# The loop over pairs of experts as a hardware loop on four engines instead of four written-out copies

## Chip, core and metric

The kernel runs on one core of a Trainium2 chip. The metric is the device time of one execution in microseconds (us), as the median of repeated runs. TensorE does the matrix products, VectorE and ScalarE the elementwise work, SyncE issues nearly all transfers; GpSimd does nothing here. Each engine has its own instruction stream, and the streams meet only in semaphores.

## The reference, cut to what matters here

The program is a two-layer backbone. What the change touches is the last part of the second layer, a mixture of experts: each of 256 tokens goes to the two best of eight experts, each with three weight matrices of 1024 x 2816 in fp32.

```
def moe_swiglu(h, router, w_gate, w_up, w_down):
    hf = h.reshape(-1, d)                                   # 256 x 1024
    top_v, top_i = lax.top_k((hf @ router), 2)
    top_w = jax.nn.softmax(top_v, axis=-1)
    gates = sum(one_hot(top_i, 8) * top_w[..., None], axis=1)
    y = zeros_like(hf)
    for e in range(8):
        y = y + gates[:, e:e + 1] * (silu(hf @ w_gate[e]) * (hf @ w_up[e])) @ w_down[e]
    return y
```

Everything ahead of it (modulation, gMLP and pooling mixer, dense SwiGLU, two attentions) and the final RMSNorm are the same in both kernels.

## The kernel before

Each fp32 operand is split in two parts, hi and lo, so that one product is three matmuls of fp32r operands: hi x hi, hi x lo, lo x hi (`product`, lines 502 to 506). Weights travel as slabs of 128 x 2048 fp32, 1 MB each. A slab passes four engines:

- SyncE issues its transfer into one of six `raw` buffers (`load`, line 427; the transfer is line 438). It waits for the `lo_ready` semaphore, which says that the slab six places earlier has been split.
- ScalarE copies `raw` to one of three `hi` buffers (`split_hi`, line 451). It waits for the transfer (`raw_in`) and for `slab_used`, which TensorE raises when it is through with the slab three places earlier.
- VectorE subtracts to make `lo` (`split_lo`, line 459), waiting for `hi_ready`, and raises `lo_ready`.
- TensorE waits for `lo_ready` (`slab`, line 466) and does its 12 matmuls (24 for the two narrow slabs of an expert).

An expert is 33 slabs: 22 for the gate and up projections in six column chunks (`features`), 11 for the down projection (`down_e`). In between, TensorE gathers the tokens of the next expert, turns the activations, and scatters the results of the expert before (`gather_rows`, `turn`, `scatter`); ScalarE and VectorE empty those banks. Tokens are gathered into 128 slots for each expert. A ninth pass, `expert("ninth", ...)`, takes the expert whose tokens overflow the 128 slots, whichever that is: its number is read from memory into a register, so SyncE's addresses in it are computed. After that a loop `Fori(0, OVER - 1)` with an `If` inside would take further overflows; with these inputs its body is skipped both times. Its body holds one expert.

Two tables, `slab_order` and `bank_order`, say for each stage how often it is repeated and which count every semaphore reaches. For the stage "moe" they hold one body of two experts (66 slabs), repeated NE // 2 = 4 times. All waits are written with the turn `it`: the count is a constant plus `it` times what one body adds, as in line 469, `there = n0 // SPL + 1 + it * (per // SPL)`. In the kernel before, `it` is a Python number, so every count is a constant in the program, and the body stands there four times for each engine. Where `it` is a register, `load` adds one wait more (lines 434 to 436), for `hi_ready` against a constant:

```
                sp.wait_ge(lo_ready[freed[1] % SPL], freed[1] // SPL + 1 + it * (per // SPL))
                if not isinstance(it, int):

                    sp.wait_ge(hi_ready, freed[1] + 1)
```

VectorE also uses the number of the expert as an address: line 1356 reads a column of `posn`, line 1415 one of `gate_e`.

Of the kernel before, what the change touches and what calls it, by code (L numbers as in the profile page):

```python
# [50 lines left out]
NE = 8  # L51
# [177 lines left out]
def build(nc, a, out):  # L229
# [38 lines left out]
    with ExitStack() as ctx:  # L268
# [158 lines left out]
        def load(sp, stage, key, src, it=0):  # L427

            _, per, slot, _, _, freed = slabs[stage, key]
            if freed and freed[0] == "direct":  # L430
                sp.wait_ge(direct_done, freed[1] + 1)
            elif freed:
# [4 lines that stand above are left out]
            _, k, f = src.shape  # L437
            sp.dma_start(view(raw[slot], (k, f)), src).then_inc(raw_in[slot], 16)
# [20 lines left out]
        def split_lo(dve, stage, key, size=SLAB, it=0):  # L459

            n0, per, slot, _, _, _ = slabs[stage, key]
            dve.wait_ge(hi_ready, n0 + 1 + it * per)
            nc.vector.tensor_tensor(lo[n0 % SPL][:, 0:size], raw[slot][:, 0:size], hi[n0 % SPL][:, 0:size].bitcast(F32),  # L463
                                    ALU.subtract).then_inc(lo_ready[n0 % SPL], 1)
# [32 lines left out]
        def await_emptied(eng, stage, key, it=0, lag=0):  # L497

            b, r, per = banks[stage, key][:3]
            eng.wait_ge(bank_emptied[b], r + 1 - lag * per + it * per)  # L500
# [71 lines left out]
        def _(sp):  # L572
# [53 lines left out]
            def expert(stage, w, e, it):  # L626
                for s, (kind, _, ks, fs) in enumerate(ES):
                    load(sp, stage, (w, s), mw[kind][bass.ds(e, 1), :, ks, fs].rearrange("e p k f -> p (e k) f"), it)
            for it in range(NE // 2):
                for w in range(2):  # L630
                    expert("moe", w, it * 2 + w, it)
            sp.wait_ge(routed, 1)
# [12 lines left out]
        def _(act):  # L645
# [215 lines left out]
            def gathered(stage, w, it=0):  # L861

                for h in range(2):
                    gathered_hi(stage, w, h, it)
                for h in range(2):
                    gathered_lo(stage, w, h, it)
                gathered_places(stage, w, it)
# [15 lines left out]
            def expert(st, w, it):  # L883

                for s in range(33):
                    split_hi(act, st, (w, s), it=it)
                    if s == 2 and st == "moe":
                        out_hi(st, 1 - w, it, lag=1 - w)
                    if s == 2 and st == "ninth":
                        out_hi("moe", 1, NE // 2 - 1)  # L890
                    if s % 4 == 0 and 4 <= s <= 20:
                        silu_e(st, w, s // 4 - 1, it)
                    if s in (10, 14, 18, 22, 24):
                        act_hi(st, w, (s - 10) // 4 if s < 24 else 4, it)
                    if s == 23:
                        silu_e(st, w, 5, it)
                    if s in (25, 26) and st == "moe":
                        gathered_hi(st, w, s - 25, it)
                    if s == 27:
                        act_hi(st, w, 5, it)  # L900
                    if s in (28, 29) and st == "moe":
                        gathered_lo(st, w, s - 28, it)
                    if s == 30 and st == "moe":
                        gathered_places(st, w, it)
            gathered("first", 1)
            for it in range(NE // 2):
                expert("moe", 0, it)
                expert("moe", 1, it)
            expert("ninth", 0, 0)
# [17 lines left out]
        def _(dve):  # L927
# [468 lines left out]
            def act_lo(st, w, c, first, it):  # L1396
                n_ = 4 if c < 5 else 2
                b = full(dve, st, ("t", w, c), it)
                hi_there(st, first + c, it)
                emptied(V.tensor_tensor(aTl[:, 4 * c:4 * c + n_, :], b[:, 0:n_ * P].rearrange("p (k s) -> p k s", k=n_),  # L1400
                                        aTh[:, 4 * c:4 * c + n_, :].bitcast(F32), ALU.subtract), st, ("t", w, c))
# [16 lines left out]
            def expert(st, w, it):  # L1418

                first = {"moe": 8 * w + 2, "ninth": 8 * NE + 2, "over": 0}[st]  # L1420
                for s in range(33):
                    splits(st, (w, s), it=it)
                    if s == 2 and st == "moe":
                        out_lo(st, 1 - w, it, 8 * w, lag=1 - w)
                    if s == 2 and st == "ninth":
                        out_lo("moe", 1, NE // 2 - 1, 16)
                    if s in (6, 10, 14, 18, 22):
                        act_e(st, w, (s - 6) // 4, it)
                    if s in (6, 7) and st != "over":
                        add_out(st, w, it * 2 + w if st == "moe" else NE, range(2 * s - 12, 2 * s - 10), it)  # L1430
                    if s in (10, 14, 18, 22, 24):
                        act_lo(st, w, (s - 10) // 4 if s < 24 else 4, first, it)
                    if s == 12 and st == "moe":
                        place(0, 1 - w, it * 2 + (w + 1))
                    if s == 23:
                        act_e(st, w, 5, it)
                    if s == 27:
                        act_lo(st, w, 5, first, it)
            for it in range(NE // 2):
                expert("moe", 0, it)  # L1440
                expert("moe", 1, it)
            expert("ninth", 0, 0)
# [36 lines left out]
        def _(pe):  # L1479
# [391 lines left out]
            def expert(st, w, it):  # L1871
                if st == "over" or w == 1:
                    for key in (("xl", 1 - w, 1), ("pt", 1 - w)):
                        await_emptied(pe, st, key, it)
                elif st == "moe":
                    for key in (("xl", 1, 1), ("pt", 1)):
                        await_emptied(pe, st, key, it, lag=1)
                else:
                    for key in (("xl", 1, 1), ("pt", 1)):
                        await_emptied(pe, "moe", key, NE // 2 - 1)  # L1880
                for c in range(6):
                    features(st, "g", w, c, it)
                    features(st, "u", w, c, it)
                    if c == 0 and st == "moe":
                        for h in range(2):
                            await_emptied(pe, st, ("d", 1 - w, h), it, lag=1 - w)
                        scatter(st, w, 1 - w, it)
                    if c == 0 and st == "ninth":
                        for h in range(2):
                            await_emptied(pe, "moe", ("d", 1, h), NE // 2 - 1)  # L1890
                        scatter(st, 0, 1)
                    if c:
                        turn(st, w, c - 1, it)
                down_e(st, w, it)
# [4 lines left out]
            gather(0, "first", 1, 0, 2)  # L1899
            for key in (("xl", 1, 1), ("pt", 1)):  # L1900
                await_emptied(pe, "first", key)
            for it in range(NE // 2):
                expert("moe", 0, it)
                expert("moe", 1, it)
            expert("ninth", 0, 0)
# [34 lines left out]
```

## Time and profile before

| | |
|---|---|
| median of 3 runs | 1822.49 us (1821.17 to 1822.96) |
| the profiled execution | 1821.17 us, of which its span, first to last instruction, is 1819.4 us |
| mean granted TensorE clock | 0.958 of full speed |
| busy | TensorE 93%, VectorE 76%, ScalarE 50% |
| DMA | 426 MB, mean 234 GB/s |
| the stage of the change | about 901.6 to 1797 us: eight experts, then the ninth pass |

The times in a row are microseconds from the start of the span, unless marked ns. PE is TensorE's matmuls, PEld its weight loads, DVE VectorE, ACT ScalarE, SP SyncE. PEldq, ACTq, DVEq and SPq are what the sequencers of TensorE, ScalarE, VectorE and SyncE do themselves: branches, register arithmetic, semaphore waits that stand alone, issues of transfers. They are not counted as busy. A matmul's recorded duration overlaps the next one's; what a matmul takes in a stream is the distance of two starts.

### The profile page before, as it was taken

How to read it: one execution, taken by the hardware profiler on the slowest of the kernel's cores; microseconds unless marked ns; L12 is line 12 of the kernel's file. 1: busy time of each engine (PE TensorE's matmuls, PEld its weight loads, DVE VectorE, ACT ScalarE, POOL GpSimd, SP SyncE). 2: the span in 40 equal slices, each digit the busy share in tenths (PEclk: the TensorE clock that was granted, in tenths of full speed). 3: DMA queues.
4: the chain of work that ended last, by engine and by line, in shares of the span. 5: the costliest groups of instructions: out<-in, count | busy, mean ns of one | idle time of the engine just before them, and what ended most of it. 6: DMA issues, size and time to landing. Idle time of an engine off the chain costs nothing.

```text
span 1819.4 us, 20970 instructions
## 1 busy us (share of the span) xinstructions
PE 1689.4 (93%) x8417; PEld 1387.7 (76%) x8418; DVE 1388.9 (76%) x1442; ACT 910.9 (50%) x837; POOL 0.2 (0%) x4
## 2 busy tenths in 40 slices
PE   4988999999999797797799999999999999999995
PEld 1876777788888596466688888888888888888884
DVE  5858657776777845674488988889798989888896
ACT  5431232211122334332477777777677777777773
POOL 0000000000000000000000000000000000000000
PEclk9988999999999898899699999999999999999998
DMA  9533334444567132100299999999999999999992
GB/s 352 195 136 126 113 127 149 139 163 161 170 223 242 53 117 70 47 1 24 68 337 342 358 346 343 358 337 360 344 341 350 354 335 357 341 348 356 334 366 88
DMA packets 214552, 426.32 MB, mean 234 GB/s; under 512 B 8186, under 2 KB 64028, under 8 KB 214452
## 3 DMA queue, kind: packets, MB, share of 16 engines
q1 hardware_dynamic: 210218, 420.37, 65.9%
q10 hardware_dynamic: 4234, 4.57, 0.8%
q8 instruction: 69, 1.13, 0.3%
q14 instruction: 31, 0.25, 0.0%
HBM read 423.86 MB, written 1.05 MB: 234 GB/s over the span
## 4 chain that ended last, share of the span: by engine, by line
PE 88%; DVE 6%; ACT 2%; issue 1%; DMA 1%; SPq 1%; DVEq 0%; ACTq 0%
PE bank L504 26%; PE bank L506 25%; PE bank L505 25%; PE bank L1740 2%; PE bank L1795 2%; PE bank L1729 2%; DVE lo L463 2%; PE bank L1834 1%; PE bank L1515 1%; DMA raw<-in_ada_w_dram 1%; PE bank L1746 1%; PE bank L1509 1%; ACT hi L457 1%; PE bank L1868 0%; PE bank L1869 0%
## 5 line engine op out<-in xcount | busy, mean ns | idle before, releaser
L463 DVE TENSOR_TENSOR lo<-raw,hi 128x2048 fp32r<-128x2048 f32 x361 | 820.8, 2282 | 199.4 <-ACT hi L457 198.0
L457 ACT ACTIVATE hi<-raw 128x2048 fp32r<-128x2048 f32 x361 | 689.7, 1912 | 474.9 <-PE bank L506 454.3
L504 PE MATMUL bank<-hi,xgh 128*128 128x512 f32 (+1 forms) x864 | 328.8, 381 | 5.0 <-DVE lo L463 5.0
L506 PE MATMUL bank<-hi,xgl 128*128 128x512 f32 (+1 forms) x864 | 325.3, 377 | 0.0
L505 PE MATMUL bank<-lo,xgh 128*128 128x512 f32 (+1 forms) x864 | 325.3, 377 | 0.0
L504 PEld LDWEIGHTS bank<-hi,xgh 128*128 128x128 f32 x864 | 163.0, 189 | 36.6 <-issue 5.2
L506 PEld LDWEIGHTS bank<-hi,xgl 128*128 128x128 f32 x864 | 163.1, 189 | 33.0
L505 PEld LDWEIGHTS bank<-lo,xgh 128*128 128x128 f32 x864 | 163.1, 189 | 31.3
L504 PE MATMUL bank<-hi,aTh 128*128 128x512 f32 x396 | 159.0, 402 | 0.0
L506 PE MATMUL bank<-hi,aTl 128*128 128x512 f32 x396 | 154.7, 391 | 0.0
L505 PE MATMUL bank<-lo,aTh 128*128 128x512 f32 x396 | 154.4, 390 | 0.0
L1023 DVE SCALAR_TENSOR_TENSOR acc<-raw,cs,acc 128x512 f32<-128x512 f32 x216 | 146.6, 746 | 1.4
L504 PE MATMUL bank<-Hhi,hi 128*128 128x512 f32 x352 | 140.6, 399 | 2.8 <-issue 2.8
L506 PE MATMUL bank<-Hhi,lo 128*128 128x512 f32 x352 | 138.8, 394 | 0.0
L505 PE MATMUL bank<-Hlo,hi 128*128 128x512 f32 x352 | 138.5, 393 | 0.0
L506 PEld LDWEIGHTS bank<-hi,aTl 128*128 128x128 f32 x396 | 74.3, 188 | 16.6
L504 PE MATMUL bank<-hi,Hhi 128*128 128x256 f32 (+1 forms) x256 | 83.2, 325 | 2.7 <-DVE lo L463 2.7
L505 PEld LDWEIGHTS bank<-lo,aTh 128*128 128x128 f32 x396 | 74.6, 188 | 13.9
L504 PEld LDWEIGHTS bank<-hi,aTh 128*128 128x128 f32 x396 | 74.5, 188 | 13.6
L505 PE MATMUL bank<-lo,Hhi 128*128 128x256 f32 (+1 forms) x256 | 81.3, 318 | 0.0
L506 PE MATMUL bank<-hi,Hlo 128*128 128x256 f32 (+1 forms) x256 | 81.3, 318 | 0.0
L504 PEld LDWEIGHTS bank<-Hhi,hi 128*128 128x128 f32 x352 | 66.6, 189 | 17.8 <-issue 3.7
(315 smaller groups left out, 2188.8 us busy)
## 6 DMA issues: line engine op xcount, KB each, us to landing
raw<-in_moe_w_gate_dram SPq DMA_DIRECT2D x99, 1024.0 KB, 5.9
raw<-in_moe_w_up_dram SPq DMA_DIRECT2D x99, 1024.0 KB, 6.0
raw<-in_moe_w_down_dram SPq DMA_DIRECT2D x99, 1024.0 KB, 6.3
raw<-in_ada_w_dram SPq DMA_DIRECT2D x48, 1024.0 KB, 5.8
raw<-in_ffn_w_gate_dram SPq DMA_DIRECT2D x11, 1024.0 KB, 5.3
raw<-in_ffn_w_up_dram SPq DMA_DIRECT2D x11, 1024.0 KB, 5.3
raw<-in_ffn_w_down_dram SPq DMA_DIRECT2D x11, 1024.0 KB, 5.0
raw<-in_ab_w_in_dram SPq DMA_DIRECT2D x6, 1024.0 KB, 8.7
```

The costliest lines, as they stand in the source:

```text
L457: nc.scalar.activation(hi[n0 % SPL][:, 0:size], raw[slot][:, 0:size], ACT.Copy).then_inc(hi_ready, 1)
L463: nc.vector.tensor_tensor(lo[n0 % SPL][:, 0:size], raw[slot][:, 0:size], hi[n0 % SPL][:, 0:size].bitcast(F32), ALU.subtract).then_inc(lo_r ...
L504: nc.tensor.matmul(dst, lh, rh, start=first, stop=False, skip_group_check=True)
L505: nc.tensor.matmul(dst, lh, rl, start=False, stop=False, skip_group_check=True)
L506: return nc.tensor.matmul(dst, ll, rh, start=False, stop=last, skip_group_check=True)
L1023: ins = V.scalar_tensor_tensor(out=sum_, in0=w_, scalar=c_, in1=biased[:, place_, :] if h == 0 and i < 2 else sum_, op0=ALU.mult, op1=ALU.add)
L1509: filled(T.matmul(bank(pe, st, ("bc", cb, who))[:], ones[:], sums[:, who, :], start=True, stop=True), st, ("bc", cb, who))
L1515: ins = T.matmul(b[:, 2 * j + who:2 * j + who + 1], sums[:, who, j * P:(j + 1) * P], ones[:, 0:1], start=True, stop=True)
L1729: filled(T.matmul(bank(pe, "att", ("s", i))[:], q_, k_, start=True, stop=True), "att", ("s", i))
L1740: ins = T.matmul(b[:, 0:64], pT[:, i % 2, t * P:(t + 1) * P], val, start=(t == 0), stop=(t == 3))
L1746: ins = T.transpose(b[:, t * P:(t + 1) * P], pexp[:, (i - 1) % 2, t * P:(t + 1) * P], ident[:])
L1795: ins = T.matmul(b[:, kk * P:(kk + 1) * P], src[:, t, k * P:(k + 1) * P], Pm[:, par, t, :], start=(t == 0), stop=(t == 1))
```

## The change

In four places, one for each engine, `for it in range(NE // 2)` becomes a hardware loop over the same body. `it` is then a register. The order of the work, the buffers and the semaphores are the same.

```
             def expert(stage, w, e, it):
                 for s, (kind, _, ks, fs) in enumerate(ES):
                     load(sp, stage, (w, s), mw[kind][bass.ds(e, 1), :, ks, fs].rearrange("e p k f -> p (e k) f"), it)
-            for it in range(NE // 2):
+            with sp.Fori(0, NE // 2) as it:
                 for w in range(2):
                     expert("moe", w, it * 2 + w, it)
...
             gathered("first", 1)
-            for it in range(NE // 2):
+            with act.Fori(0, NE // 2) as it:
                 expert("moe", 0, it)
                 expert("moe", 1, it)
...
-            for it in range(NE // 2):
+            with dve.Fori(0, NE // 2) as it:
                 expert("moe", 0, it)
                 expert("moe", 1, it)
...
                 await_emptied(pe, "first", key)
-            for it in range(NE // 2):
+            with pe.Fori(0, NE // 2) as it:
                 expert("moe", 0, it)
                 expert("moe", 1, it)
```

## Rows read from the trace of the kernel before

**Rows 1.** The page's part on busy time, share of the span and instructions, TensorE

```profile
PE 1689.4 (93%) x8417; PEld 1387.7 (76%) x8418; DVE 1388.9 (76%) x1442; ACT 910.9 (50%) x837; POOL 0.2 (0%) x4
```

**Rows 2.** Stretches: length, busy us (xinstructions) PE to POOL, clock, DMA share, GB/s

```profile
999.40:1099.10 99.70, 99.70 (x486) 82.78 (x485) 85.69 (x54) 71.72 (x53) 0.00 (x0) 1.00 0.98 348
...
1103.30:1302.70 199.40, 199.40 (x969) 165.60 (x968) 171.37 (x107) 143.53 (x104) 0.00 (x0) 1.00 0.98 348
```

**Rows 3.** Who waited for whom from 899 to 1797 us: total us, times, longest

```profile
ACT hi L457 <- PE bank L506: 249.4, 283, 3.4
...
PE bank L504 <- DVE lo L463: 5.0, 1, 5.0
```

**Rows 4.** Timeline of TensorE's weight loads at the end of the sixth expert

```profile
1499.24 0.19 PEld L504 LDWEIGHTS bank<-hi,aTh 128*128 128x128 f32 x1
...
1501.96 0.19 PEld L504 LDWEIGHTS bank<-hi,xgh 128*128 128x128 f32 x1
```

**Rows 5.** Lines 470 and 477: ns min/median/max, first and last start in us

```profile
L470 PEldq EVENT_SEMAPHORE  x1: 51/51/51, 1498.6 to 1498.6; - x1
...
L477 PEldq EVENT_SEMAPHORE  x1: 51/51/51, 1498.7 to 1498.7; - x1
```

**Rows 6.** Timeline of ScalarE and VectorE in the same stretch

```profile
1494.28 1.92 ACT L457 ACTIVATE hi<-raw 128x2048 fp32r<-128x2048 f32 x1 [0.80 <-PE bank L506]
1497.00 1.92 ACT L457 ACTIVATE hi<-raw 128x2048 fp32r<-128x2048 f32 x1 [0.80 <-PE bank L506]
...
1496.23 2.29 DVE L463 TENSOR_TENSOR lo<-raw,hi 128x2048 fp32r<-128x2048 f32 x1 [0.43 <-ACT hi L457]
1498.95 2.29 DVE L463 TENSOR_TENSOR lo<-raw,hi 128x2048 fp32r<-128x2048 f32 x1 [0.43 <-ACT hi L457]
```

**Rows 7.** Branch and register instructions at lines 1912 and 1910, TensorE's queue

```profile
L1912 PEldq COMPARE_BRANCH  x2: 221/2082/3944, 1800.1 to 1805.4; - x2
...
L1910 PEldq FUSED_REGOPS  x2: 59/59/59, 1799.1 to 1804.6; - x2
L1910 PEldq ALU_OP  x2: 36/39/42, 1804.1 to 1805.7; - x2
L1910 PEldq COMPARE_BRANCH  x2: 76/159/242, 1804.3 to 1805.8; - x2
```

**Rows 8.** Register and branch instructions of ScalarE's and VectorE's queues, and line 881

```profile
L912 ACTq MOVE  x1: 39/39/39, 1797.5 to 1797.5; - x1
...
1797.53 0.60 ACT L881 ACTIVATE yeh<-bank 128x512 fp32r<-128x512 f32 x1 [0.76 <-PE bank L506]
...
L1449 DVEq COMPARE_BRANCH  x2: 50/53/56, 1804.5 to 1805.9; - x2
```

**Rows 9.** DMA queues from 1103.3 to 1302.7 us, then the whole run

```profile
q8 instruction: 8, 0.13, 0.3%
q14 instruction: 2, 0.02, 0.0%
...
q8 instruction: 69, 1.13, 0.3%
```

**Rows 10.** Line 438, four experts of the stage, then the ninth

```profile
L438 SPq DMA_DIRECT2D raw<-in_moe_w_up_dram x44: 367/368/368, 1105.1 to 1501.3; - x44
...
DMA to landing us min/median/max: 4.8/6.3/9.0
...
L438 SPq DMA_DIRECT2D raw<-in_moe_w_up_dram x11: 372/373/373, 1688.6 to 1745.4; - x11
```

**Rows 11.** Stretches around two falls of TensorE's clock

```profile
832.00:834.84 2.84, 0.57 (x4) 0.35 (x3) 2.11 (x4) 1.00 (x3) 0.00 (x0) 1.00 0.00 0
834.84:838.25 3.41, 3.41 (x10) 2.63 (x9) 0.00 (x0) 0.00 (x0) 0.00 (x0) 0.50 0.00 0
...
896.60:901.57 4.97, 0.00 (x1) 0.03 (x1) 2.44 (x2) 4.97 (x5) 0.00 (x0) 0.81 0.00 0
901.57:906.50 4.93, 4.93 (x12) 3.88 (x13) 4.93 (x4) 2.03 (x3) 0.00 (x0) 0.50 0.81 258
```

More of the change, by code:

```diff
@@ L628, in expert @@
                     load(sp, stage, (w, s), mw[kind][bass.ds(e, 1), :, ks, fs].rearrange("e p k f -> p (e k) f"), it)
-            for it in range(NE // 2):
+            with sp.Fori(0, NE // 2) as it:
                 for w in range(2):
@@ L905, in _ @@
             gathered("first", 1)
-            for it in range(NE // 2):
+            with act.Fori(0, NE // 2) as it:
                 expert("moe", 0, it)
@@ L1438, in expert @@
                         act_lo(st, w, 5, first, it)
-            for it in range(NE // 2):
+            with dve.Fori(0, NE // 2) as it:
                 expert("moe", 0, it)
@@ L1901, in _ @@
                 await_emptied(pe, "first", key)
-            for it in range(NE // 2):
+            with pe.Fori(0, NE // 2) as it:
                 expert("moe", 0, it)
```

## Prediction

> **What bounds the kernel now.** I read the page's busy part first: TensorE is busy for 93% of the span, nothing else for over 76% [rows 1]. Then the stretches. In the stage that the change touches, TensorE is busy in all of 99.70 us of an expert, at full clock, and two experts from boundary to boundary take 199.40 us; DMA is close behind, at a share of 0.98 and 348 GB/s [rows 2]. Then the waits: from 899 to 1797 us TensorE's matmuls wait once, 5.0 us before the first slab, while ScalarE waits 283 times for TensorE [rows 3]. So TensorE sets the end of this stage, and there is nothing to win in it: what the change can do is put time into TensorE's stream, or leave it alone.
>
> The reader is to see next how far each stream is ahead of its engine at the end of a body, since a branch is taken by the sequencer, not by the array. Three branches back are added for each engine (four turns), at the end of the experts 2, 4 and 6. At the end of the sixth expert TensorE's sequencer sees `lo_ready` for the last slab at 1498.6 us and stands at the first wait of the next expert at 1498.7 us [rows 5]. The array takes up the last slab at 1499.24 us, with the load of its first weights, and the next expert at 1501.96 us [rows 4]. So at 1498.7 us it has work for 3.2 us more: the sequencer is that far ahead.
>
> **The change, part by part.**
>
> Removed: nothing that an engine executes, only three of four copies of the code.
>
> The branch back on TensorE. A body of two experts is long: in 199.4 us TensorE's instruction queue moves 8 packets, 0.13 MB [rows 9]. The nearest row for a jump to code that is not at hand is the first branch of line 1912, which passes over the body of the overflow loop, one expert or half that length: it takes 3.94 us, and the next instruction (the ALU_OP of line 1910) starts at 1804.1, right behind it. The branches that follow, the one back to the head of that loop among them, take 0.24, 0.22 and 0.08 us [rows 7]. I take the long one, because after 8 packets the start of the body is the oldest code of all, where the short branches went back to code met 5 us before. Under load the fetch may take longer. Below that is nothing: a packet of instructions takes 0.3% of 16 engines x 199.4 us / 8 = 1.2 us in the loaded stage, and 0.3% x 16 x 1819.4 / 69 = 1.27 us over the whole run [rows 9]. Above, SyncE's transfers land in 4.8 to 9.0 us in this stage [rows 10], 4.2 us apart. I take 0.4 us, near the packets, since they are the same kind of transfer.
>
> Around the branch: the counter's ALU_OP before it, 0.2 us to the branch (1804.1 to 1804.3), and behind it the head of the loop and the counts of the first four waits. A step of register work takes some 0.1 us with its gap (the 0.24 us branch at 1804.3, the next instruction at 1804.6 [rows 7]); five of them, 0.5 us, and 0.1 us for the weight load. Sum for one turn: 0.2 + 3.94 + 0.4 + 0.6 = 5.1 us, less 3.2 us ahead: TensorE stands still 1.9 us. Three turns: 5.8 us. Without the 0.4 us it is 4.6 us, with 4.2 us in its place 17 us; if the branch takes 0.24 us, nothing, since 1.0 us is under 3.2 us.
>
> The Trainium skill, Runtime: NRT & Kernel Launch, section "Instruction fetch mechanics", speaks against this change: TensorE's instruction store takes 2048 instructions in blocks of 256, it is refilled in order, and a taken branch to code outside a window of two such pages has to fetch it first. The trace agrees with the 3.94 us, and not with the 0.24 us of the branch back over four blocks, which by that rule would have cost the same again. By the rule the branch cannot be a short one, and the sum stays 5.8 us.
>
> The branches back on ScalarE and VectorE. Their sequencers are less far ahead, as they do not pass a wait that isn't met: the MOVE of line 912 starts at 1797.5 us, with the copy of line 881 in front of it that had waited until 1797.53 us [rows 8]. Their code is short (the other engines' instruction queue moves 2 packets while TensorE's moves 8 [rows 9]), and VectorE's branch back in the overflow loop takes 0.05 us [rows 8]. If they too missed, at TensorE's 5.1 us: ScalarE is free of the last slab's wait at 1494.28, would be ready at 1499.4 and is wanted at 1497.00 [rows 6], 2.4 us late. VectorE likewise, 1496.23 to 1501.3 against 1498.95, beside it and not on top. `lo` is now ready 0.7 us before it is needed (1496.23 + 2.29 = 1498.52 against the weight load at 1499.24 [rows 4]), so TensorE would get the next slab 1.7 us late, less than the 1.9 us it loses by itself. Cost either way: nothing more. It is the 1.9 us that cover it.
>
> SyncE. Its transfers get register addresses, one more wait that is met, and register steps, some 0.3 us on 0.37 us for a transfer, with 2.7 us from one to the next. The ninth pass already has computed addresses: its transfers take 373 ns against 368 [rows 10]. A late branch there (5.1 us, less 2.3 us of waiting) sets transfers back 2.8 us. Six buffers give it 6 x 2.72 us, less 4.2 us from the start of a split to its end (1494.28 to 1498.52), 12.1 us; transfers land 6.3 us after their issue, at most 9.0 [rows 10], so 3.1 us or more are left. Cost nothing; without that cover, up to 2.8 us a turn.
>
> The waits with a count in a register. Each puts a register step of 0.04 to 0.06 us (0.1 us with its gap) ahead of the wait, on all four engines. It is done while the sequencer waits anyway, as TensorE waits 2.7 us for each `lo_ready`. What hides it is the 0.7 us above. Were it gone, each 0.1 us over it would be paid for 264 slabs, 26 us. I take nothing. VectorE's column addresses (six instructions an expert) lie behind splits of 2.29 us: nothing.
>
> Sum: 1821.17 (the profiled execution: span 1819.4 and 1.8 us around it) + 5.8 = 1827.0 us. The median lies 1.3 us above that execution: **1828.3 us**, 0.3% slower.
>
> **The rivals.**
>
> A: TensorE's code is still at hand. For: the branches of 0.24, 0.22 and 0.08 us. Against: 8 packets in between. Then 1822.5 us, no change.
>
> B: The clock falls, or the fetch waits behind the weights. TensorE's clock is at its upper level, 2.4 GHz, from 906.5 us to the stage's end. A stretch of 2.84 us with 0.57 us of matmuls was followed by 3.41 us at half speed (1.2 GHz), and the 4.97 us without any by 4.93 us at half [rows 11]. A pause of 1.9 us is shorter than both, but not by much. 3.41 us at half speed cost 1.7 us of work: with it after each pause, 1833.4 us; with a fetch 4.2 us longer and 2.5 us for the clock, 3 x (5.7 + 2.5) = 25 us, 1847 us.
>
> C: The register steps use up the 0.7 us of each slab. For: ScalarE, VectorE and TensorE pass a slab round in a ring, and each gets steps. Against: at most 0.1 us each, three times, and most of it ahead of a wait. It decides from 0.7 us on; at 0.8 us it costs 26 us, 1849 us.
>
> D: Faster. The half-speed stretch from 901.57 to 906.50 us costs 2.5 us of work [rows 11]. If the change shifts the entry of the stage against the clock's next rise, it could be spared. It decides only if it takes 3.7 us or more, so this stretch alone is not enough, and the branches back would have to be free as well.
>
> **How the numbers follow.** A measurement of this kernel can tell about 0.2% (3.6 us) from no change. Forecast, TensorE stands still at each of three branches and the clock holds: 0.50, 1826 to 1833 us, nearly all of it over 3.6 us. A 0.22, B 0.18, C 0.05, D 0.03, and 0.02 for what I do not see. Range 1821.5 to 1843 us: it takes in A and most of B, and leaves out C and B's end. Slower: 0.47 of the forecast's 0.50, B and C, 0.70. Same: A, the rest of the forecast and some of the unseen, 0.26. Faster: D and some of the unseen, 0.04.
>
> **What would show it.** In the changed profile: three COMPARE_BRANCH of 4 us or more on TensorE's queue about 1100, 1301 and 1503 us; a pause of about 2 us in TensorE's stream behind each; 99.7 us for every expert without one; the granted clock 1.00 there. A short branch shows A. A lower clock behind the pauses shows B. Experts longer than 99.7 us throughout, with VectorE named in TensorE's waits, show C. The step that most likely fails is the time of the fetch in a loaded stage, for which no row stands; the next is the 3.2 us of lead, if the compiled waits let the sequencer less far ahead.

## The result, and the profile after the change

| | median of 4 runs | profiled span |
|---|---|---|
| before | 1822.72 us (1821.17 to 1823.73) | 1819.4 us |
| after | 1849.31 us (1846.95 to 1855.68) | 1844.2 us |

The changed kernel is slower: ratio 1.0152, 95% interval 1.0120 to 1.0185. The prediction was 1828.3 us (1821.5 to 1843), so the direction was right and the size was not: 26.6 us were lost, where 5.8 had been forecast. Over all 15 executions of the kernel after the median is 1848.6 us. One of the ten executions of the kernel with one branch back, below, took 4303.6 us, has no trace, and stands outside its ratio. All ratios compare executions taken together, so they are not exactly the quotients of the medians beside them.

The stretch of the stage first (length, then busy us and instructions of each engine, clock, DMA share, GB/s). The first line is all of it, the next ones go through the first branch back and the start of the turn behind it, the last two are the clock behind the other two branches.

```profile
901.53:1822.37 920.84, 904.20 (x4322) 747.53 (x4322) 769.58 (x475) 649.04 (x469) 0.00 (x0) 0.99 0.94 332
1113.45:1310.65 197.20, 197.20 (x958) 163.37 (x956) 166.50 (x103) 143.25 (x103) 0.00 (x0) 1.00 0.95 334
1102.89:1103.71 0.82, 0.00 (x1) 0.00 (x1) 0.82 (x1) 0.78 (x1) 0.00 (x0) 1.00 1.15 392
1104.21:1108.96 4.75, 0.01 (x2) 0.01 (x1) 3.74 (x4) 1.60 (x3) 0.00 (x0) 0.75 1.02 375
1108.96:1113.45 4.49, 4.49 (x11) 3.52 (x12) 0.00 (x0) 0.00 (x0) 0.00 (x0) 0.50 0.78 287
...
1316.72:1321.66 4.94, 4.94 (x12) 3.88 (x13) 0.00 (x0) 0.00 (x0) 0.00 (x0) 0.50 0.69 257
...
1524.62:1529.87 5.25, 5.25 (x12) 4.14 (x13) 0.00 (x0) 0.15 (x1) 0.00 (x0) 0.50 0.68 250
```

The same 4322 matmuls took 895.92 us before, with no idle time in between:

```profile
901.57:1797.49 895.92, 895.92 (x4322) 742.99 (x4322) 769.15 (x475) 640.86 (x463) 0.00 (x0) 1.00 0.96 341
```

So the stage is 24.9 us longer. Of these 920.84 - 904.20 = 16.6 us are idle time of TensorE. The other 8.3 us are slower work: 4.49 + 4.94 + 5.25 = 14.7 us at half clock (1.2 GHz) do the work of 7.3 us; the 0.9 us left were not traced further; a matmul ahead of a pause is recorded longer (0.39 and 0.50 us at the first branch) than the 0.23 us from one start to the next in the stream, and that is of this size. Between the disturbances TensorE is busy in all of 197.20 us at clock 1.00, as in [rows 2].

Now the waits from 899 to 1830 us (who waited for whom: total, times, longest), the answer to [rows 3]. "issue" means that nothing the profile shows held the instruction back; it simply had not been sent.

```profile
PEld bank L505 <- issue: 14.3, 3, 5.1
PE bank L505 <- issue: 13.4, 3, 4.7
PEld bank L504 <- DVE lo L463: 6.5, 1, 6.5
PE bank L504 <- DVE lo L463: 6.3, 1, 6.3
...
PE bank L504 <- issue: 3.3, 3, 1.3
```

Three waits at line 504, 3.3 us together, and three at line 505, 13.4 us. There are two pauses behind each branch back, not one. The timeline of TensorE's weight loads shows how close together they lie:

```profile
1102.28 0.19 PEld L506 LDWEIGHTS bank<-hi,aTl 128*128 128x128 f32 x1
1103.71 0.19 PEld L504 LDWEIGHTS bank<-hi,xgh 128*128 128x128 f32 x1 [1.24 <-issue]
1108.95 0.29 PEld L505 LDWEIGHTS bank<-lo,xgh 128*128 128x128 f32 x1 [5.06 <-issue]
```

One weight load and one matmul stand between the two; with the four register steps ahead of them, that is six instructions from the head of the loop. The clock falls inside the second pause already (0.75 on average from 1104.21 to 1108.96 us). The branches themselves, on TensorE's queue (ns min/median/max, first and last start in us; the short one is the last, which is not taken):

```profile
L1902 PEldq COMPARE_BRANCH  x4: 79/4112/4562, 1099.2 to 1723.0; - x4
```

Starts 1099.2 and 1723.0 are three turns apart: 207.9 us a turn, 8.5 more than the 199.4 of [rows 2]. Last, ScalarE's and TensorE's entry into the stage, first after, then before:

```profile
895.55 0.38 ACT L858 ACTIVATE PT<-bank 128x256 fp32r<-128x256 f32 x1
895.95 1.28 ACT L457 ACT_TABLE_LOAD   x1
897.24 3.71 ACT L457 ACTIVATE hi<-raw 128x2048 fp32r<-128x2048 f32 x2
```

```profile
896.85 0.38 ACT L858 ACTIVATE PT<-bank 128x256 fp32r<-128x256 f32 x1
897.11 3.71 ACT L457 ACTIVATE hi<-raw 128x2048 fp32r<-128x2048 f32 x2
```

The head of ScalarE's loop has a table load that the written-out code had not. It stands ahead of the first copy, and so TensorE's first wait grew from 5.0 us [rows 3] to 6.3. In these two executions the work ahead of the stage happened to end 1.3 us earlier after the change, which hides it in the comparison of the spans. Inside the loop there are three more such loads at line 457; TensorE has no wait there for VectorE that would show them.

### The profile page after: what moved, and what is told of

Its sections match the earlier page's. It is cut to its first block, busy times and chain, and to the rows that moved or that the text cites. A ratio compares the mean times of both kernels' runs of the same rounds, so it can differ in the third digit from the quotient of the medians.

```text
span 1844.2 us, 22480 instructions
## 1 busy us (share of the span) xinstructions
PE 1697.8 (92%) x8417; PEld 1391.6 (75%) x8418; DVE 1389.3 (75%) x1442; ACT 920.5 (50%) x844; POOL 0.2 (0%) x4
## 4 chain that ended last, share of the span: by engine, by line
PE 87%; DVE 6%; ACT 3%; issue 2%; DMA 1%; SPq 1%; DVEq 0%; ACTq 0%
PE bank L504 26%; PE bank L505 25%; PE bank L506 25%; PE bank L1740 2%; PE bank L1795 2%; PE bank L1729 2%; DVE lo L463 2%; PE bank L1834 1%; PE bank L1515 1%; DMA raw<-in_ada_w_dram 1%; PE bank L1746 1%; PE bank L1509 1%; ACT hi L457 1%; PE bank L1868 0%; PE bank L1869 0%
## 5 line engine op out<-in xcount | busy, mean ns | idle before, releaser
L457 ACT ACTIVATE hi<-raw 128x2048 fp32r<-128x2048 f32 x361 | 689.3, 1912 | 490.1 <-PE bank L506 469.4
L505 PE MATMUL bank<-lo,xgh 128*128 128x512 f32 (+1 forms) x864 | 328.5, 380 | 13.4 <-issue 13.4
L506 PEld LDWEIGHTS bank<-hi,aTl 128*128 128x128 f32 x396 | 74.3, 188 | 16.6
```

What stands on the lines that cost most here:

```text
L457: nc.scalar.activation(hi[n0 % SPL][:, 0:size], raw[slot][:, 0:size], ACT.Copy).then_inc(hi_ready, 1)
L505: nc.tensor.matmul(dst, lh, rl, start=False, stop=False, skip_group_check=True)
L506: return nc.tensor.matmul(dst, ll, rh, start=False, stop=last, skip_group_check=True)
```

## The experiments

The theory after the comparison: (1) all of the loss but 1.3 us is TensorE's code. A branch back costs two fetches one after the other, each some 4 us: one for the block of code at the loop's head, one for the block behind it, since the head lies near the end of its block. The long second pause lets the clock fall. (2) 1.3 us are the table load. Rivals: after a taken branch the code always comes in two pieces; the register counts or the branches of the other engines hold up slabs; the loop as such is slower.

**Where the head of TensorE's loop lies in its block.** TensorE's code comes in blocks of 256 instructions: in the kernel before, a turn of about 2041 instructions moved 8 packets of 16 KB [rows 9]. `head_slot` sets the place of the loop's first instruction in its block, 0 being the block's start. Two kernels with one edit each against the kernel after (in the second the place is 236):

```
-            with pe.Fori(0, NE // 2) as it:
+            with pe.bass.Fori(0, NE // 2, engines=[pe.engine], head_slot={pe.engine: 0}) as it:
```

> TensorE's loop is placed so that its first instruction stands at the start of a block of 256 instructions; nothing else changes against the kernel after. In the trace after, each branch back is followed by two pauses of the array: one of 0.82, 1.10 and 1.34 us for the branch itself, and behind the first matmul, six instructions on, one of 4.74, 4.48 and 4.16 us. My theory: the second pause is a second fetch, wanted at once because the head of the loop lies a few instructions ahead of the end of a block. Then it is gone here: TensorE stands still some 1.1 us per turn, the clock keeps its upper level, and the time is 1822.7 + 3.3 + 1.3 (a table load on ScalarE at the entry) = 1827 us. Rival: whatever is fetched after a taken branch comes in two pieces, wherever the head lies; then the second pause stays and the time stays 1849 us.

> The same, but the loop of TensorE starts 20 instructions ahead of the end of a block: some eight matmuls instead of one stand between the head and the end of the block. My theory: the second fetch is still wanted, but 1.6 us of work lies ahead of it, so the second pause is 2.5 to 3.2 us instead of 4.2 to 4.7; with first pauses of 1.1 us, 1822.7 + 1.3 + 3.3 + 8.6 = 1836 us, more if the clock still falls (2.5 us each at most, 1843 us). Rival (two pieces wherever the head lies): the second pause comes behind the first matmul as before, 1849 us. A second rival, that placing a loop costs time by itself: slower than 1849 us.

Measured: head at place 0, 1827.86 us, ratio to the kernel before 1.0018 (0.9995 to 1.0041). Head at place 236, 1841.52 us, ratio 1.0097 (1.0067 to 1.0127). The branches and the waits with the head at 0 (five branches now, since one of 0.31 us jumps to the placed head):

```profile
L1902 PEldq COMPARE_BRANCH  x5: 79/4049/4177, 896.1 to 1701.6; - x5
```

```profile
PEld bank L504 <- issue: 4.0, 3, 1.4
PE bank L504 <- issue: 2.7, 3, 1.0
```

and the waits with the head at 236:

```profile
PEld bank L506 <- issue: 10.5, 3, 3.5
PE bank L506 <- issue: 9.2, 3, 3.1
...
PE bank L504 <- issue: 3.3, 3, 1.2
```

The branch back still takes 4.05 to 4.18 us with the head at 0, but the second pause is gone, and after the rise at its entry the clock holds through the stage. With the head 20 instructions ahead of the boundary the second pause comes at another line (506) and is 3.05 to 3.09 us instead of 4.5, since some eight matmuls lie ahead of it; the clock fell at two of the three. The rival of two pieces wherever the head lies has fallen. Placing the loop's head gave back 21 of the 26.6 us.

**Which engine's loop.** TensorE's turns written out and the other three engines looping, then the reverse:

```
-            with pe.Fori(0, NE // 2) as it:
+            for it in range(NE // 2):
```

> TensorE's four turns are written out as before the change; ScalarE, VectorE and SyncE keep their hardware loops. My theory: nearly all of the loss is TensorE's code. Then 1822.7 + 1.3 = 1824.0 us, the 1.3 us from the table load that stands at the head of ScalarE's loop and delays the first copy of a slab (it starts 1.69 us behind the copy of the tokens in the kernel after, 0.26 us behind it in the kernel before). Rival (the counts held in registers on the three other engines, or their branches, hold the slabs up): 1830 to 1849 us.

> TensorE alone keeps its hardware loop; ScalarE, VectorE and SyncE are written out as before the change. My theory: 24.9 us of the loss are TensorE's and the 1.3 us of the table load fall away: 1822.7 + 24.9 = 1847.6 us, within 1.5 us of the kernel after. The first copy of a slab starts 0.3 us behind the copy of the tokens. Rival (the loops of the other engines carry a part of the loss, by later slabs behind each branch): 1830 to 1843 us.

Measured: TensorE written out 1822.75 us, ratio 1.0002 (0.9980 to 1.0024); TensorE alone looping 1848.89 us, ratio 1.0156 (1.0139 to 1.0173). All of the loss that can be measured is TensorE's. In the kernel after, the branches back of ScalarE, VectorE and SyncE took 0.04 to 0.07 us. With TensorE written out, its only wait in the stage is the first, 6.4 us instead of 5.0:

```profile
PE bank L504 <- DVE lo L463: 6.4, 1, 6.4
```

Its stage ends at 1798.69 us instead of 1797.49, and the span is 1820.6 instead of 1819.4: the table load is worth 1.2 us in the trace, too little for the times to tell.

**One branch back instead of three.** TensorE's loop makes two turns, the other two are written out behind it:

```
-            with pe.Fori(0, NE // 2) as it:
+            with pe.Fori(0, 2) as it:
                 expert("moe", 0, it)
                 expert("moe", 1, it)
+            for it in range(2, NE // 2):
+                expert("moe", 0, it)
+                expert("moe", 1, it)
```

> TensorE's loop makes two turns and the two others are written out: one branch back instead of three. My theory, a price per branch back (4.0 us of branch, 4.7 us of second fetch, 2.2 us of clock, less 3 us of lead): one third of 24.9 us, so 1822.7 + 1.3 + 8.0 = 1832 us, 1831 to 1833. Here the head lies at the same place in its block as in the kernel after, if nothing ahead of it changes. Rival (the loss comes with the loop as a whole, by its register counts): half of the turns run in the loop, 1836 us, and no more than 1.3 us of it lies at the branch.

Measured: 1831.0 us, ratio 1.0035 (1.0014 to 1.0055), span 1827.7, 8.3 us over that of before. The two pauses were 2.3 and 3.6 us (the branch took 5.49 us here), and the clock fell once. One branch back costs a third of the 24.9 us that three cost; the rival, a loss that comes with the turns in the loop (1836 us), has fallen.

**Asking for the code ahead of the branch.** The loop has an option that puts one instruction, a BranchPrefetchHint for its own branch back, at the head of each turn. First alone, then with the head at place 0:

```
-            with pe.Fori(0, NE // 2) as it:
+            with pe.bass.Fori(0, NE // 2, engines=[pe.engine], hint_back_edge=True) as it:
```

> One instruction more at the head of each of TensorE's turns, a BranchPrefetchHint for the loop's branch back, which asks for the block at the loop's head before the branch is taken; the place of the head is otherwise left as it is. My theory of two separate fetches: the branch gets short (under 0.3 us instead of 3.95 to 4.56), but the fetch of the block behind the head stays (the gap of 4.2 to 4.7 us, now one instruction earlier); with 3 us of lead left to cover it, pauses of 1 to 1.8 us per turn, no fall of the clock: 1822.7 + 1.3 + 4 = 1828 us. Rival: the hint does nothing for a fetch in this loaded stage: 1849 us, branches of 4 us. Second rival: the shift of the head by one instruction already moves it across something: then less than 1828 us.

> Both together on TensorE: the head of the loop at the start of a block, and the hint. My theory: the branch is under 0.3 us and there is no second fetch, so the array never stops; 1822.7 + 1.3 = 1824.0 us, and the 1.3 us is ScalarE's table load at the entry. Rival (hint without effect): 1827 us. Rival (the hint takes the place of another fetch, so that the code ahead of the branch is late): over 1827 us, with a new pause ahead of each branch.

Measured: hint alone 1827.08 us, ratio 1.0042 (1.0027 to 1.0057); hint and head at 0, 1830.25 us, ratio 1.0068 (1.0039 to 1.0096). The first number is near the expectation, and its reason was wrong: no turn had a second pause. The second missed by 6 us; in these few executions the two kernels do not differ clearly. Branches and waits of the hint alone:

```profile
L1902 PEldq COMPARE_BRANCH  x4: 80/224/260, 1099.8 to 1698.1; - x4
```

```profile
PEld bank L506 <- issue: 3.2, 1, 3.2
PE bank L506 <- issue: 2.8, 1, 2.8
```

The branch back is short, 0.22 to 0.26 us. In place of three pauses there is one, at 1702.25 us, behind the branch at 1698.1 that is not taken: on the way out of the loop the next block is not there. With the head at 0 it lasted 3.15 us and the clock fell, with the hint alone it lasted 2.81 and the clock held (one execution of each). First the stretches of head at 0, then those of the hint alone:

```profile
1703.26:1706.41 3.15, 0.00 (x1) 0.00 (x0) 2.73 (x2) 2.52 (x3) 0.00 (x0) 0.86 1.05 378
1706.41:1712.34 5.93, 5.93 (x14) 4.67 (x15) 1.92 (x3) 1.20 (x1) 0.00 (x0) 0.50 0.94 347
```

```profile
1702.25:1705.06 2.81, 0.00 (x1) 0.00 (x0) 2.39 (x2) 2.52 (x3) 0.00 (x0) 1.00 1.05 394
1705.06:1712.00 6.94, 6.94 (x30) 5.63 (x31) 4.55 (x4) 3.37 (x2) 0.00 (x0) 1.00 0.87 315
```

3.15 + 5.93 / 2 = 6.1 us is what the second expectation missed by (6.25 us): the rival "the hint takes the place of another fetch" was right, but behind the branch that leaves the loop, not ahead of each branch. Where the head lies in its block with the hint alone was not set. It must have moved to the first places of a block: the kernel fetched nothing in three turns, which below goes only with a body that touches at most eight blocks, and 2042 instructions do that from the places 0 to 6 alone. So the second rival of that expectation, the shift of the head, is what happened, and the hint by itself is read from the pair with the head at 0: branches back of 4.05 to 4.18 us without it, 0.22 to 0.26 us with it.

**Branch in the middle of a block.** The hint, and the head at place 135, so that the branch has 128 instructions of its block ahead of it and 127 behind; then the same with ScalarE's turns written out as well:

```
-            with pe.Fori(0, NE // 2) as it:
+            with pe.bass.Fori(0, NE // 2, engines=[pe.engine], hint_back_edge=True,
+                              head_slot={pe.engine: 135}) as it:
```

> The hint as before, and the head of TensorE's loop at place 135 of its block, so that the branch back (2041 instructions on) lies in the middle of a block: 128 instructions of its block ahead of it, 127 behind. With the hint alone no turn had a pause, but the way out of the loop had one of 2.81 us, and 3.15 us with the head at place 0, some ten instructions behind the branch that is not taken. My theory: that pause is the fetch of the block behind the branch, which the hint had displaced and which starts at the branch; with 127 instructions in hand it is hidden, as is the hinted fetch with 128 instructions ahead. Then no pause from 902 us to the stage's end, the clock holds, and the time is 1822.7 + 1.2 (the table load at ScalarE's loop head, as in the run with TensorE written out) = 1823.9 us. Rival: the hint's displacement lasts to the end of the block however far that is; then a pause of 3 to 4.7 us at the end of that block, 1827 us.

> The same with ScalarE's four turns written out as before the change; TensorE, VectorE and SyncE loop. My theory: the table load at the entry is gone, the first copy of a slab starts 0.3 us behind the copy of the tokens instead of 1.7, and the time is that of the kernel before, 1822.5 us. It would be the best of the kernels with loops and beats neither measurably nor by the trace the kernel before. Rival: 1824 us, if the 1.2 us has another cause.

Measured: 1820.97 us, ratio 0.9995 (0.9971 to 1.0019), and 1822.18 us, ratio 0.9998 (0.9979 to 1.0016). The times cannot tell the table load; the rival of a pause at the end of the block has fallen. The stretch from the clock's rise to 1795 us, of the first and then of the second:

```profile
905.21:1795.00 889.79, 889.79 (x4307) 738.36 (x4306) 764.50 (x473) 646.01 (x465) 0.00 (x0) 1.00 0.97 343
```

```profile
905.21:1795.00 889.79, 889.79 (x4307) 738.20 (x4305) 763.64 (x471) 638.22 (x460) 0.00 (x0) 1.00 0.96 342
```

TensorE never stops and the clock never falls in it. With ScalarE written out the first copy again follows the copy of the tokens directly, and TensorE's wait at the entry is 4.84 us instead of 6.26:

```profile
893.95 0.60 ACT L853 ACTIVATE xgl<-bank 128x512 fp32r<-128x512 f32 x1 [0.29 <-PE bank L1795]
894.44 0.38 ACT L858 ACTIVATE PT<-bank 128x256 fp32r<-128x256 f32 x1
894.71 3.71 ACT L457 ACTIVATE hi<-raw 128x2048 fp32r<-128x2048 f32 x2
```

So a looped kernel loses nothing measurable against the written-out one, and none beats it measurably.

**How much code TensorE keeps.** Why was the head of the loop gone at all? Three kernels with the head at place 0, without the hint, and with shorter bodies. `thin` leaves out the second matmul of a product where it is true (that part of the result is then missing):

```
             nc.tensor.matmul(dst, lh, rh, start=first, stop=False, skip_group_check=True)
-            nc.tensor.matmul(dst, lh, rl, start=False, stop=False, skip_group_check=True)
+            if not thin:
+                nc.tensor.matmul(dst, lh, rl, start=False, stop=False, skip_group_check=True)
```

> TensorE's loop at the start of a block, without a hint, and the second of the three matmuls of each product left out in the eight experts (hi x lo: that part of the result is missing). The body is 1481 instructions instead of 2041, 5.8 blocks of 256 instead of 8.0. Only the branch is read here, not the time, since the slabs then wait for the transfers. Theory: TensorE keeps some eight blocks of code, so that the loop's first block is still there when the body is shorter: branches back under 0.3 us and next to no packets on the instruction queue during the loop. Rival (only a window of two blocks is kept, whatever the body's length): 4 us per branch as before, and one packet per block.

> As the run before, with that matmul left out in the down projections of both experts and in the gate and up projections of the first of the two only: the body is 1673 instructions, 6.5 blocks, and touches seven. Only the branch is read. Theory of some eight kept blocks: under 0.3 us, since seven and the next one that is fetched ahead are eight. Rival of a two-block window: 4 us. A theory of fewer kept blocks (four, as the overflow loop's body of one expert showed at least): short in neither this run nor the one before.

> As the two runs before, with the second matmul of a product left out in the down projections alone: the body is 1865 instructions, 7.3 blocks, and touches eight, with no hint. Only the branch is read. Bodies that touch six and seven blocks had short branches and no packets in the later turns; the full body (2041 instructions from the start of a block, eight blocks touched) had branches of 4.05 to 4.18 us and nine packets a turn. Theory: eight blocks are kept, and the one fetched ahead, the ninth, takes the place of the loop's first; then this body too misses, 4 us per branch and nine packets a turn. Rival (it is the number of instructions that counts, or the ninth is only fetched close to the end of the eighth): short branches, since the branch lies 183 instructions ahead of that end.

Measured, one execution of each, the branch rows of the three in this order (of the five branches the first, 0.32 us, jumps to the placed head and the last, 0.08 us, is not taken):

```profile
L1903 PEldq COMPARE_BRANCH  x5: 76/208/321, 909.7 to 1617.5; - x5
```

```profile
L1903 PEldq COMPARE_BRANCH  x5: 76/213/318, 910.6 to 1623.6; - x5
```

```profile
L1903 PEldq COMPARE_BRANCH  x5: 79/5792/6342, 899.5 to 1658.4; - x5
```

| kernel | body | blocks touched | packets on TensorE's instruction queue | taken branch back |
|---|---|---|---|---|
| thin everywhere | 1481 | 6 | 0 from 1090 to 1600 us | 0.21 to 0.24 us |
| thin in part | 1673 | 7 | 0 from 1090 to 1600 us | 0.21 to 0.24 us |
| thin in the down projections | 1865 | 8 | 9 per turn | 5.79 to 6.34 us |
| full, head at 0 | 2041 | 8 | 9 per turn | 4.05 to 4.18 us |
| full, hint, head at 0 | 2042 | 8 | 0 from 1100 to 1698 us | 0.22 to 0.26 us |
| full, hint, head at 135 | 2042 | 9 | 9 per turn | 0.34 to 0.37 us |
| full, as in the kernel after | 2041 | 9 | 10 per turn | 3.95 to 4.56 us |

The packets per turn, of the thin kernel with eight blocks (1282 to 1472 us) and of the kernel after (1300 to 1508 us):

```profile
q8 instruction: 9, 0.15, 0.3%
```

```profile
q8 instruction: 10, 0.16, 0.3%
```

The theories of two and of four kept blocks have fallen, and so has the rival of the third run, which had expected short branches for 1865 instructions; its branches missed, and took longer than the 4 us expected. Without the hint, a kernel that misses fetches one block more in each turn than the body touches. The reading that fits all seven rows: eight blocks fit; the ninth, fetched ahead while TensorE works in the eighth, takes the place of the loop's first. The hint keeps that ninth away (from 1062 to 1098 us, in the last block of the first turn, the kernel with the head at 0 moves one packet without the hint and none with it), which is why with it a body of eight blocks needed no packet at all in three turns; its nine-block form (head at 135) fetched nine a turn, all of them in time. A limit by the number of instructions alone does not fit, since 1865 missed and 2042 with the hint did not.

## Why the prediction was wrong

- **TensorE sets the end, no slack**: right. Its 16.6 us of pauses and 7.3 us of lost clock lie in the stage's length one to one.
- **One turn's branch at 3.94 + 0.4 us**: right. Measured 3.95, 4.27 and 4.56 us, mean 4.26 against 4.34.
- **The lead of 3.2 us and 1.2 us of steps around the branch, pause 1.9 us**: the first pause was 0.82, 1.10 and 1.34 us, mean 1.1. The size was off, mostly by the lead: the branch begins 3.7 us before the array runs dry (1099.2 to 1102.89), where the sum had 3.2 less 0.2 = 3.0 us; behind it the matmul starts after 0.54 us, near the 0.6 us of the sum, and the 0.4 us for the loaded stage were about right. For this pause the sum was 2.5 us too long over three turns (5.8 against 3.3).
- **The step that failed: a turn was charged with one fetch.** "Sum for one turn" ended with the first weight load of the new turn. The block behind the head is a second fetch, which in every turn started only after the branch had ended, and here it was wanted six instructions on: 4.74, 4.47 and 4.16 us, 13.4 us in all. Nothing in the sum asked where in its block the loop's head lies. Moving the head alone took these 13.4 us away, and with them the clock's fall.
- **The clock holds**: wrong, and as a consequence. A pause of some 1 us did not lower it; 4.2 us and more did, for 7.3 us of work. The price of 2.5 us a turn in rival B was right (7.3 / 3 = 2.4).
- **Rival B** gave 1847 us for its far end, and 1849.3 was measured. Its mechanism was one fetch made 4.2 us longer by the weights under way. That is not what happened: there were two fetches. The first was hardly slower than in the tail of the kernel before (3.95 to 4.56 against 3.94 us [rows 7]), the second took 5.1 to 5.8 us from the branch's end to the matmul behind it. That B's number came so close is luck. It had been given 0.18 for its whole span, and the range left its end out.
- **Rival A**, code at hand: fell, for the reason given against it (8 packets in between). It was closer than it looked: it holds for a body that touches seven blocks, and with the hint for one that touches eight. The Trainium skill, Runtime: NRT & Kernel Launch, "Instruction fetch mechanics", was right on 2048 instructions in blocks of 256, and right that this branch would miss; its window of two pages does not agree with bodies of six and seven blocks whose branches back took 0.21 to 0.24 us and whose later turns had no packets.
- **The other engines cost nothing**: their branches were short (0.04 to 0.07 us), and with TensorE written out the kernel was as fast as before. Right but for the table load at ScalarE's loop head, 1.2 us at the entry, which the list of added instructions did not have. The Trainium skill, ScalarE activation tables: per-element evaluation and per-set limits, section "Table sets in the compiler and the runtime", says that the compiler places table loads per block; the trace agrees, with eight of them in the stage's loop (four turns, lines 457 and 871) where the written-out code had one. The 1.283 us of each, and that the other seven stayed hidden, are this case's rows.
- **Rival C**, register steps: fell. From 1113.45 to 1310.65 us TensorE has no idle time at all, and the turns of the kernel with the hint are (1698.1 - 1099.8) / 3 = 199.4 us apart, as in [rows 2].
- **Rival D**, a shorter half-speed stretch at the entry: it ran from 901.53 to 905.2 us instead of 901.57 to 906.5 [rows 11], some 0.6 us of work, and decided nothing.

Still open: why the compiled head of the loop lay where it did (nothing in the source sets it), and why the fetches differ. The traces say where the difference lies. From the start of a branch to the start of its block's packet on TensorE's instruction queue it took 1.5 us (kernel after, first branch), 3.0 us (one branch back) and 3.9 us (1865 instructions, first branch), against 1.6 us in the tail of the kernel before; from the packet's start to the branch's end 2.5, 2.5, 2.5 and 2.3 us. So the branches of 3.95 to 6.34 us differ by the wait for the packet to start, and the packet itself is no slower. Whether the weights under way cause that wait was not tried by itself.

## What to carry to other kernels

A hardware loop on a TensorE bound kernel is priced by its code: count the instructions of the body, and if it touches eight blocks of 256 or more, charge each branch back with a fetch (4 to 6 us in this stage, less the lead), and with a second one if the head lies near the end of a block. Then either let the body touch seven blocks at most, or hint the branch back and put it in the middle of a block, with enough work on both sides to cover a fetch. Count what the compiler adds at a loop's head too, such as a table load on ScalarE.

## What was not expected of the hardware

- After a taken branch that misses, the next block is fetched only once the first has come: packets start at 1100.7, 1106.5 and 1112.4 us on TensorE's instruction queue behind the branch at 1099.2, which ends at 1103.2. They are 5.8 and 5.9 us apart in a stage where a packet itself takes 1.3% of 16 engines x 15 us / 3 = 1.0 us:

```profile
q8 instruction: 3, 0.05, 1.3%
```

- Pauses of TensorE of 2.81, 3.05, 3.08, 3.09 and 3.15 us brought no fall, 3.4 us at half clock, no fall, a fall to half clock within the pause, and 5.9 us at half clock behind it. The length of a pause alone does not say whether the clock falls. The second and third are of the kernel with its head at 236, and so is that of 3.09 us:

```profile
1108.01:1111.06 3.05, 0.00 (x0) 0.00 (x1) 2.24 (x3) 0.00 (x0) 0.00 (x0) 1.00 1.03 383
1111.52:1114.94 3.42, 3.42 (x10) 2.64 (x9) 0.20 (x1) 1.91 (x1) 0.00 (x0) 0.50 0.79 292
```

```profile
1519.48:1522.56 3.08, 0.00 (x1) 0.00 (x1) 2.18 (x3) 0.00 (x0) 0.00 (x0) 1.00 1.01 374
1522.56:1529.00 6.44, 6.44 (x28) 5.19 (x29) 2.75 (x2) 4.30 (x3) 0.00 (x0) 1.00 0.50 187
```
